# Reordering three places of a long mixer-and-feed-forward kernel: a causal attention's end, a linear attention's two rounds, and the last feed-forward phase

## The chip, the cores and the metric

The kernel runs on one core of one Trainium2 chip. A core has TensorE (PE in the profile; PEld is its weight load), VectorE (DVE), ScalarE (ACT), GpSimd (POOL) and SyncE (SP), which here issues almost all transfers. Each engine runs its own list of instructions in order; they meet only at semaphores (counters that one engine raises and another waits for). The metric is the device time of one execution in microseconds, the median of several runs.

## The reference

Two transformer blocks work on 512 tokens of width 1024, all in f32. The change lies in the second block:

```python
n = rms_norm_2(h, norm1_g);  proj = n @ w_in          # split into mq, mk, mv, gq, gk, gv, g_low, g_out, two gates
y_moba = moba_attention(mq, mk, mv, t5_bias)            # 8 heads of 64, causal, softmax with a T5 bias
log_a  = log_sigmoid(g_low @ gate_up + gate_bias) / 16
y_gla  = gla_attention(gq, gk, gv, log_a)               # 4 heads, keys 128, values 256, chunks of 64
y_gla  = rms_norm_2(y_gla, out_norm_g) * silu(g_out)
mixed  = sigmoid(gate_moba) * (y_moba @ w_branch_moba) + sigmoid(gate_gla) * (y_gla @ w_branch_gla)
h = h + mixed @ w_out
h = h + square(relu(rms_norm_2(h, norm2_g) @ w_up)) @ w_down       # 4096 hidden columns
```

With 512 tokens and blocks of 256, the selective attention comes to plain causal attention.

## The kernel before, in words

**Products.** Every f32 operand of a large product is kept as two parts: a high part rounded to fp32r (ACT copies it) and the rest, the low part (DVE or POOL subtracts). One product is then three matmuls into one PSUM bank, high by high, high by low, low by high: the helper `three` (lines 2328 to 2330). Activations lie transposed, 128 features by 512 tokens, so that a weight tile of 1024x128 is a product of 8 k-steps, 24 matmuls. A weight tile is loaded by SP into one of two slots of `w_raw` (`load_tile`, line 586), ACT makes `w_hi` (line 877), POOL makes `w_lo` (line 769), into one of four slots. `lo_done` counts finished low parts, `tile_done` finished products. No planner orders the work: the order of each engine is the order in which the code writes it out.

**Causal attention** (`scores`, `turn`, `output`, `gate`, `branch` on PE). For each head m and each query block q of 128: `scores` (two matmuls, lines 2789 and 2792, banks 4 and 5), DVE scales, adds the bias and takes the maximum (lines 1988, 1990), ACT exponentiates (1279), DVE divides (1995, 1996), `turn` transposes the probabilities on PE (2804, banks 6 and 7), ACT and DVE copy them out as high and low parts (1284, 2001). When all four blocks are turned, `output(m)` multiplies by the values (2814, 2815, bank m % 2); ACT and DVE take the result out as `y_hi`, `y_lo` (1290, 2008, 2009), counted by `o_lo`. Products that depend on none of this, the tiles of `gate_moba` (`gate(c, k0, k1)`, banks 2 and 3), are cut into k-steps and laid between the steps of the heads to keep PE busy. After head 7 come the four `branch` products (y_moba by w_branch_moba: two banks, 4*o + j, 4 k-steps each, so 24 matmuls; k-step k reads heads 2k and 2k+1), with the 16 matmuls of `g_low` (2866, 2867) between the second and third. These need `low_hi_and_lo`, which ACT and DVE make after ACT has copied the last gate tile, split a weight tile and applied eight sigmoids (lines 1258, 877, 1317, 1320, 2041).

**Linear attention.** A hardware loop of two rounds, two heads in each, `with pe.Fori(0, 2) as i`; ACT and DVE have loops of their own over the same rounds. A round computes four tiles of gq and gk (banks 4, 5, 0, 1), the values, the attention, and four tiles of g_out (`out_gate(j)`, banks 6, 7, 4, 5; ACT drains each by a SiLU and raises `y_s`), then transposes the output rows (`turn_rows`, 2931) and waits for the round's last `y_s` (4 and 8) as its last step. Behind the loop comes a loop of two rounds for the eight tiles of gate_gla (banks 4 to 7).

**Feed-forward.** Eight phases of 512 hidden columns. A phase has four `up` tiles (24 matmuls each; ACT applies relu and square) and a 2x2 block product in seven multiplications, M1, M2, M6, M5, M7, M4, M3 in PE's order (`down(n, x, p)`: two row blocks p, 6 matmuls each, bank `ff_bank(x, p)`: M1, M6, M7 share banks 0 and 1, M5 and M3 share 2 and 3). Operands of M5, M6, M7 and M3 are sums of blocks: M5 = a21 + a22, M6 = M5 - a11, M7 = a11 - a21, M3 = a12 - M6 (DVE's `hidden_sum`, counted by `f_sum`). ACT makes each high part (`hidden_hi`), DVE each low part (`hidden_lo`), in place of the sum where there was one. DVE adds each finished bank to the output rows (`add`, line 2273), each waiting for the one before (`f_add`), and M6, M7 and M3 on PE wait for the adds that free their banks: M6 for M1's, M7 for M6's, M3 for M5's. In the last phase M2 and M4 have banks and adds of their own, and SP stores finished rows (line 750). DVE does all four sums first, then all low parts, then the adds.

Of the kernel before, what the change touches and what calls it, by code (L numbers as in the profile page):

```python
# [20 lines left out]
P = 128  # L21
# [4 lines left out]
KC = D // P  # L26
# [5 lines left out]
HEADS = 8  # L32
# [10 lines left out]
MH = 8  # L43
# [92 lines left out]
def build(nc, d):  # L136
# [6 lines left out]
    with ctx:  # L143
# [14 lines left out]
        WH = at("w_hi", 56, [P, 4, KC * P], f32r)  # L158
# [140 lines left out]
        def bank(b, n=T, o=0):  # L299
            return PB[:, b * T + o:b * T + o + n]  # L300
# [172 lines left out]
        def ff_bank(x, p):  # L473

            return {M2: 4, M4: 6, M5: 2, M3: 2}.get(x, 0) + p

        def added(n, x, p=1):

# [394 lines left out]
        def _(act):  # L873
# [605 lines left out]
            def hidden_hi(n, x):  # L1479

                act.wait_ge(f_sq, HID * n + (2 if x == M1 else 4))
                if x in (M6, M5, M7, M3):
                    act.wait_ge(f_sum, 4 * n + {M5: 1, M6: 2, M7: 3, M3: 4}[x])
                plain = {M1: HF[:, 0:2, HALVES[0]], M2: HF[:, 2:4, HALVES[0]], M4: HF[:, 2:4, HALVES[1]]}
                act.activation(HAH[:, x, :, :], plain[x] if x in plain else HS[:, x, :, :], ACT.Copy).then_inc(f_hi, 1)

# [32 lines left out]
        def _(v):  # L1519
# [718 lines left out]
            def hidden_sum(n, x):  # L2238

                v.wait_ge(f_sq, HID * n + 4)  # L2240
                if x == M6 or x == M3:
                    v.wait_ge(f_sum, 4 * n + {M6: 1, M3: 2}[x])
                slot = lambda y: HS[:, y, :, :]
                if x == M5:
                    ins = v.tensor_tensor(slot(M5), a21, a22, ALU.add)
                elif x == M6:
                    ins = v.tensor_tensor(slot(M6), slot(M5), a11, ALU.subtract)
                elif x == M7:
                    ins = v.tensor_tensor(slot(M7), a11, a21, ALU.subtract)
                else:  # L2250
                    ins = v.tensor_tensor(slot(M3), a12, slot(M6), ALU.subtract)
                ins.then_inc(f_sum, 1)

            def hidden_lo(n, x):

                v.wait_ge(f_hi, 7 * n + x + 1)
                if x in (M6, M5, M7, M3):
                    v.wait_ge(f_sum, 4 * n + 4)
                src = {M1: a11, M2: a12, M4: a22}[x] if x in (M1, M2, M4) else HS[:, x, :, :]
                v.tensor_tensor(HAL[:, x, :, :], src, f(HAH[:, x, :, :]), ALU.subtract).then_inc(f_lo2, 1)  # L2260

# [2 lines left out]
            def add(n, x, p, m, half):  # L2264

                v.wait_ge(f_mm, ff_no(n, x, p))
                if n == 0 and x == M1 and p == 0:
                    v.wait_ge(r_copied, COPIED0 + 2 * TT)
                    v.wait_ge(c_rstd, RSTD0 + 3)
                if counted[0]:  # L2270
                    v.wait_ge(f_add, ADDED0 + counted[0])
                cols = slice(half * T, (half + 1) * T)
                v.scalar_tensor_tensor(ROWS[:, m, cols], bank(ff_bank(x, p)), RSC[:, m:m + 1], ROWS[:, m, cols], ALU.mult, ALU.add)\  # L2273
                    .then_inc(f_add, 1)
                counted[0] += 1
# [13 lines left out]
            for n in range(PHASES):  # L2289
                nxt = n < PHASES - 1  # L2290
                hidden_lo(n, M1)
                for x in (M5, M6, M7, M3):
                    hidden_sum(n, x)
                for x in range(1, 7):
                    hidden_lo(n, x)
                for p in range(2):
                    add(n, M1, p, p, 0)
                if not nxt:
                    for p in range(2):
                        add(n, M2, p, p, 0)  # L2300
                for p in range(2):
                    add(n, M6, p, p, 1)
                for p in range(2):
                    add(n, M5, p, p + 2, 1)
                if nxt:
                    down_sum(n + 1, M5)
                    down_sum(n + 1, M6)
                for p in range(2):
                    add(n, M7, p, p + 2, 0)
                    add(n, M7, p, p + 2, 1)  # L2310
                if nxt:
                    down_sum(n + 1, M7)
                    down_sum(n + 1, M4)
                else:
                    for p in range(2):
                        add(n, M4, p, p + 2, 0)
                for p in range(2):
                    add(n, M3, p, p, 1)
                if nxt:
                    for x in VECTOR_LO:  # L2320
                        low(n + 1, x)
# [3 lines left out]
        def _(pe):  # L2325
# [503 lines left out]
            for m in range(MH):  # L2829
                scores(m, 2, 4)  # L2830
                if m:
                    held = 4 if m < MH - 1 else 2
                    gate(m, held - 1, held)
                    output(m - 1)
                turn(m, 0)
                turn(m, 1)
                if m < MH - 1:
                    scores(m + 1, 0, 1)
                if m < MH - 1:
                    gate(m, 4, KC)  # L2840
                else:
                    gate(m, 2, 5)
                turn(m, 2)
                if m < MH - 1:
                    scores(m + 1, 1, 2)
                if m < MH - 1:
                    gate(m + 1, 0, 3 if m < MH - 2 else 1)
                turn(m, 3)
            gate(MH - 1, 5, 7)
            output(MH - 1)  # L2850
            gate(MH - 1, 7, KC)

            def branch(j):
                pe.wait_ge(lo_done, BM + j + 1)
                for o in range(2):
                    for k in range(4):
                        s = slice(2 * P * k + P * o, 2 * P * k + P * (o + 1))
                        mm = three(bank(4 * o + j), WH[:, j, s], WL[:, j, s], YH[:, k, :], YL[:, k, :], k == 0, k == 3)
                mm.then_inc(tile_done, 1)

            pe.wait_ge(o_lo, HEADS + MH)
            branch(0)
            branch(1)
            pe.wait_ge(l_lo, 1)
            for k in range(KC):
                pe.matmul(bank(7), LWS[:, k, :], UH[:, k, :], start=k == 0, stop=False)
# [9 lines left out]
                pe.wait_ge(bm_e, 2 * h + 1)  # L2876
                pe.matmul(bank(h), GUS[:, h * DK:(h + 1) * DK], GLS[:], start=True, stop=True).then_inc(l_up, 1)

            with pe.Fori(0, 2) as i:
                def attention(hh):  # L2880

                    n = 2 * i + hh
# [59 lines left out]
                        mm.then_inc(tile_done, 1)  # L2942

                for j in range(4):
                    if j == 2:
                        pe.wait_ge(l_abs, GH)
                        pe.wait_ge(on_done, 4 * i + 1)
                    product(tile_no(GK, i, j, 12), j, UH, UL, out=qk_bank(j))
# [28 lines left out]
                out_gate(3)  # L2977
                turn_rows(0)
                turn_rows(1)
                pe.wait_ge(y_s, 4 * i + 4)  # L2980

            with pe.Fori(0, 2) as i:
                for j in range(4):
                    if j == 2:
                        pe.wait_ge(go_rt, GH)
                    product(tile_no(GG, i, j), j, UH, UL, out=4 + j)
# [107 lines left out]
```

## Time and profile before

| | us |
|---|---|
| median of 3 runs | 1302.81 (1301.05 to 1306.74) |
| the profiled execution | 1301.05 |
| its span, first to last instruction | 1299.2 |
| PE busy in it | 1279.2 (98%) |
| DVE, ACT, POOL busy | 813.6, 657.0, 443.9 |
| DMA | 135.37 MB, mean 104 GB/s |

Busy times are of one execution; 1.85 us of its time lie outside the span. The stages that the change touches: causal attention from about 545 to 650 us of the span, the linear attention's rounds from 666 to 831 us, the last feed-forward phase's seven multiplications from 1273 us to the end. Matmul rows of PE overlap: a 128x512 matmul has a modelled duration of 0.39 us, while the next one starts about 0.23 us after it.

### The profile page before, as it was taken

To read this page: it belongs to the slowest core of one execution; us is meant where nothing else is said; L and a number is where in the kernel's file an instruction comes from. 1 tells how busy PE (TensorE), PEld (TensorE's weight loads), DVE (VectorE), ACT (ScalarE), POOL (GpSimd) and SP (SyncE) were. 2 spreads that over 40 slices of the span, in tenths; PEclk is the share of its full clock that TensorE was granted. 3 is DMA by queue.
4 is the path that set the end of the run, shared out by engine and by line. 5 is a ranking of instruction groups with operands and counts; after the bars stand their busy time and mean duration, and the time that the engine had idled before them with its cause. 6 is when DMAs were issued, how large, how long until landed. Compare 5 with 4: busy or idle time off the path is not lost.

```text
span 1299.2 us, 17513 instructions
## 1 busy us (share of the span) xinstructions
PE 1279.2 (98%) x6553; PEld 1066.6 (82%) x6553; DVE 813.6 (63%) x1215; ACT 657.0 (51%) x1074; POOL 443.9 (34%) x203
## 2 busy tenths in 40 slices
PE   8999999999999999999999999999999999999998
PEld 4688788889988888877689889888888888888886
DVE  1795788764935448778647325405448768667685
ACT  5553777844533354666654534633355544445341
POOL 0233011137432494422234333344563322332300
PEclk9999999999999999999999999999999999999999
DMA  9972001076332152321223322233255243332301
GB/s 349 313 238 74 11 23 33 18 242 198 90 91 65 45 167 81 100 63 49 64 65 98 82 81 68 72 102 97 82 161 159 84 126 102 101 111 81 114 1 65
DMA packets 181397, 135.37 MB, mean 104 GB/s; under 512 B 10154, under 2 KB 154651, under 8 KB 181324
## 3 DMA queue, kind: packets, MB, share of 16 engines
q1 hardware_dynamic: 181122, 134.34, 34.1%
q8 instruction: 46, 0.75, 0.3%
q14 instruction: 27, 0.22, 0.1%
q10 hardware_dynamic: 202, 0.06, 0.0%
HBM read 129.66 MB, written 4.72 MB: 103 GB/s over the span
## 4 chain that ended last, share of the span: by engine, by line
PE 88%; DVE 4%; ACT 3%; issue 2%; DMA 2%; POOL 1%; SPq 0%; DVEq 0%; ACTq 0%; POOLq 0%
PE psum L2328 27%; PE psum L2330 26%; PE psum L2329 26%; PE psum L2540 2%; DMA ada_w<-in_w_ada 1%; PE psum L2386 1%; PE psum L2530 1%; PE psum L2531 1%; POOL w_lo L769 1%; PE psum L2804 1%; PE psum L2792 1%; PE psum L2479 1%; ACT w_hi L877 0%; DMA w_raw<-in_w_in 0%; PE psum L2815 0%
## 5 line engine op out<-in xcount | busy, mean ns | idle before, releaser
L769 POOL TENSOR_TENSOR w_lo<-w_raw,w_hi 128x1024 fp32r<-128x1024 f32 x148 | 382.4, 2589 | 662.8 <-ACT w_hi L877 621.0
L2328 PE MATMUL psum<-u_hi,w_hi 128*128 128x512 f32 (+1 forms) x704 | 267.0, 379 | 1.7 <-ACT gated L1399 1.5
L2330 PE MATMUL psum<-u_hi,w_lo 128*128 128x512 f32 (+1 forms) x704 | 260.8, 370 | 0.0
L2329 PE MATMUL psum<-u_lo,w_hi 128*128 128x512 f32 (+1 forms) x704 | 260.7, 370 | 0.0
L877 ACT ACTIVATE w_hi<-w_raw 128x1024 fp32r<-128x1024 f32 x148 | 155.6, 1056 | 80.4 <-PE psum L2330 37.1
L2328 PE MATMUL psum<-y_hi,w_hi 128*128 128x512 f32 x416 | 162.2, 390 | 1.4 <-DVE y_lo L2009 1.4
L2329 PE MATMUL psum<-y_lo,w_hi 128*128 128x512 f32 x416 | 161.9, 389 | 0.0
L2330 PE MATMUL psum<-y_hi,w_lo 128*128 128x512 f32 x416 | 161.9, 389 | 0.0
L2328 PEld LDWEIGHTS psum<-u_hi,w_hi 128*128 128x128 f32 x704 | 132.7, 188 | 28.1 <-issue 4.4
L2330 PEld LDWEIGHTS psum<-u_hi,w_lo 128*128 128x128 f32 x704 | 132.7, 188 | 23.2
L2329 PEld LDWEIGHTS psum<-u_lo,w_hi 128*128 128x128 f32 x704 | 132.8, 189 | 20.6 <-issue 0.2
L2273 DVE SCALAR_TENSOR_TENSOR out_rows<-psum,row_rstd,out_rows 128x512 f32<-128x512 f32 x100 | 75.0, 750 | 39.5 <-PE psum L2330 34.8
L2328 PEld LDWEIGHTS psum<-y_hi,w_hi 128*128 128x128 f32 x416 | 78.1, 188 | 17.9 <-DVE y_lo L2009 1.8
L2330 PEld LDWEIGHTS psum<-y_hi,w_lo 128*128 128x128 f32 x416 | 78.1, 188 | 16.1
L2329 PEld LDWEIGHTS psum<-y_lo,w_hi 128*128 128x128 f32 x416 | 78.1, 188 | 16.1
L2328 PE MATMUL psum<-down_hi,hidden_hi 128*128 128x512 f32 x224 | 87.3, 390 | 2.7 <-DVE hidden_lo L2260 2.1
L2330 PE MATMUL psum<-down_hi,hidden_lo 128*128 128x512 f32 x224 | 87.2, 389 | 0.0
L1468 ACT ACTIVATE stage<-psum 128x512 f32<-128x512 f32 x32 | 19.0, 593 | 66.7 <-PE psum L2330 66.7
L2328 PEld LDWEIGHTS psum<-down_hi,hidden_hi 128*128 128x128 f32 x224 | 42.0, 188 | 12.2 <-issue 3.5
L1495 ACT ACTIVATE down_hi<-down_sum 128x1024 fp32r<-128x1024 f32 x24 | 24.6, 1057 | 53.9 <-DVE down_sum L2222 53.3
L2329 PE MATMUL psum<-down_lo_set,hidden_hi 128*128 128x512 f32 x128 | 49.8, 389 | 0.0
L793 POOL TENSOR_TENSOR w_lo<-w_raw,w_hi 128x768 fp32r<-128x768 f32 x8 | 14.8, 1846 | 102.4 <-ACT w_hi L981 102.4
(498 smaller groups left out, 2583.3 us busy)
## 6 DMA issues: line engine op xcount, KB each, us to landing
w_raw<-in_w_in SPq DMA_DIRECT2D x52, 512.0 KB, 3.8
w_raw<-in_w_up SPq DMA_DIRECT2D x32, 512.0 KB, 4.1
down_set<-in_w_down SPq DMA_DIRECT2D x32, 512.0 KB, 4.8
ada_back<-in_w_ada SPq DMA_DIRECT2D x7, 2048.0 KB, 10.3
w_raw<-in_fno_w_in SPq DMA_DIRECT2D x16, 512.0 KB, 4.0
ada_w<-in_w_ada SPq DMA_DIRECT2D x3, 2048.0 KB, 15.3
w_raw<-in_mla_w_in SPq DMA_DIRECT2D x11, 512.0 KB, 5.2
w_raw<-in_mla_w_out SPq DMA_DIRECT2D x8, 512.0 KB, 4.3
```

The costliest lines, as they stand in the source:

```text
L769: pool.tensor_tensor(WL[:, j, :], RAW[:, j % 2, :], f(WH[:, j, :]), ALU.subtract).then_inc(lo_done, 1)
L793: pool.tensor_tensor(WL[:, h % 4, 0:768], RAW[:, h % 2, 0:768], f(WH[:, h % 4, 0:768]), ALU.subtract).then_inc(lo_done, 1)
L877: act.activation(WH[:, j, :], RAW[:, j % 2, :], ACT.Copy).then_inc(hi_done, 1)
L1468: act.activation(E[:, t % 2, :], bank(up_bank(n, j)), ACT.Relu).then_inc(f_r, 1)
L1495: act.activation(WDH[:, x, :, :], down_raw(n, x)[:], ACT.Copy).then_inc(d_hi2, 1)
L2273: v.scalar_tensor_tensor(ROWS[:, m, cols], bank(ff_bank(x, p)), RSC[:, m:m + 1], ROWS[:, m, cols], ALU.mult, ALU.add)\
L2328: pe.matmul(out, ah, bh, start=first, stop=False, skip_group_check=more)
L2329: pe.matmul(out, ah, bl, start=False, stop=False, skip_group_check=more)
L2330: return pe.matmul(out, al, bh, start=False, stop=last, skip_group_check=more)
L2386: mm = pe.matmul(ada_row_bank(q)[0:2, :], CACT[:, k, :], AQ[q][:, k, :], start=k == 0, stop=k == KC - 1)
L2479: mm = pe.matmul(bank(5, 2, 2 * (4 * r + b)), ada_sum(r)[:, b * P:(b + 1) * P], ONES[:, 0:2], start=True, stop=True)
L2540: mm = pe.transpose(bank(2, P, k * P), PA[:, q % 2, k * P:(k + 1) * P], IDENT[:])
```

## The change

Three places, all of them order or waits; every product, sum and copy is still there once.

- **Last feed-forward phase.** DVE's order in the last phase becomes: sum M5, low M2, sum M6, sum M3, low M6, the two adds of M1, sum M7, low M5, M7, M4, M3, and then the adds as before. The numbers that ACT and DVE wait for follow the new order (`summed`); the low part of M6, made in place, waits for sum M3, the others for all four sums. The phases before are unchanged.
- **Causal attention.** In head 0, two of the gate tile's k-steps move ahead of the next head's first score block. In head 7 the gate tile's last three k-steps run ahead of `turn(7, 3)`. Behind it come the k-steps of the branch product that read heads 0 to 5: nine matmuls (tile 0, bank 0), then `output(7)`, then nine each for bank 4 and bank 5, then the wait for head 7's low part and the 21 other matmuls of tiles 0 and 1.
- **Linear attention.** PE's loop is written out twice (`for i in range(2)`), so that its waits are on constants. The wait for the round's last two SiLUs moves from the round's end to the products that write the drained banks: `y_s` 3 and 4 ahead of the second round's first two tiles, 7 ahead of the gate loop, 8 ahead of its second tile.

```diff
+        def summed(n, x):
+            return 4 * n + ((M5, M6, M3, M7) if n == PHASES - 1 else (M5, M6, M7, M3)).index(x) + 1
...
 # ACT, hidden_hi
-                    act.wait_ge(f_sum, 4 * n + {M5: 1, M6: 2, M7: 3, M3: 4}[x])
+                    act.wait_ge(f_sum, summed(n, x))
 # DVE, hidden_sum and hidden_lo
-                    v.wait_ge(f_sum, 4 * n + {M6: 1, M3: 2}[x])
+                    v.wait_ge(f_sum, summed(n, M5 if x == M6 else M6))
-                    v.wait_ge(f_sum, 4 * n + 4)
+                    v.wait_ge(f_sum, summed(n, M3) if n == PHASES - 1 and x == M6 else 4 * n + 4)
 # DVE, in the loop over the phases
+                else:
+                    hidden_sum(n, M5)
+                    hidden_lo(n, M2)
+                    hidden_sum(n, M6)
+                    hidden_sum(n, M3)
+                    hidden_lo(n, M6)
+                    for p in range(2):
+                        add(n, M1, p, p, 0)
+                    hidden_sum(n, M7)
+                    for x in (M5, M7, M4, M3):
+                        hidden_lo(n, x)
...
 # PE, causal attention
                 turn(m, 0)
                 turn(m, 1)
+                if m == 0:
+                    gate(m, 4, 6)
                 if m < MH - 1:
                     scores(m + 1, 0, 1)
                 if m < MH - 1:
-                    gate(m, 4, KC)
+                    gate(m, 4 if m else 6, KC)
                 else:
                     gate(m, 2, 5)
                 turn(m, 2)
+                if m == MH - 1:
+                    gate(m, 5, KC)
...
                 turn(m, 3)
-            gate(MH - 1, 5, 7)
-            output(MH - 1)
-            gate(MH - 1, 7, KC)
+            def branch_half(j, o, k0, k1):
+                for k in range(k0, k1):
+                    s = slice(2 * P * k + P * o, 2 * P * k + P * (o + 1))
+                    mm = three(bank(4 * o + j), WH[:, j, s], WL[:, j, s], YH[:, k, :], YL[:, k, :], k == 0, k == 3)
+                return mm
...
+            pe.wait_ge(lo_done, BM + 1)
+            pe.wait_ge(o_lo, HEADS + MH - 1)
+            branch_half(0, 0, 0, 3)
+            output(MH - 1)
+            pe.wait_ge(s_max, M0 + 4 * MH)
+            branch_half(0, 1, 0, 3)
+            pe.wait_ge(lo_done, BM + 2)
+            branch_half(1, 1, 0, 3)
             pe.wait_ge(o_lo, HEADS + MH)
-            branch(0)
-            branch(1)
+            branch_half(0, 0, 3, 4)
+            branch_half(0, 1, 3, 4).then_inc(tile_done, 1)
+            branch_half(1, 0, 0, 4)
+            branch_half(1, 1, 3, 4).then_inc(tile_done, 1)
...
 # PE, linear attention
-            with pe.Fori(0, 2) as i:
+            for i in range(2):
...
                 for j in range(4):
+                    if i and j < 2:
+                        pe.wait_ge(y_s, 3 + j)
...
                 turn_rows(1)
-                pe.wait_ge(y_s, 4 * i + 4)
-
+            pe.wait_ge(y_s, 7)
             with pe.Fori(0, 2) as i:
                 for j in range(4):
+                    if j == 1:
+                        pe.wait_ge(y_s, 8)
```

## Rows read from the trace of the kernel before

**Rows 1.** Page, parts 1 and 2: busy time by engine; clock in 40 slices.
```profile
PE 1279.2 (98%) x6553; PEld 1066.6 (82%) x6553; DVE 813.6 (63%) x1215; ACT 657.0 (51%) x1074; POOL 443.9 (34%) x203
...
PEclk9999999999999999999999999999999999999999
```

**Rows 2.** Waits of PE: who was waited for; us in total, times, longest.
```profile
PE psum L2328 <- DVE hidden_lo L2260: 2.1, 1, 2.1
...
PE psum L2328 <- ACT gated L1399: 1.5, 2, 0.8
...
PE psum L2328 <- DVE gv_lo L2110: 0.8, 1, 0.8
```

**Rows 3.** Timeline, head 0: start, duration, engine, line, tiles [idle before <- releaser].
```profile
557.82 0.44 PE L2804 MATMUL psum<-ident,m_probs 128*128 128x128 f32 x2 [0.17 <-DVE m_probs L1996]
...
559.15 0.30 PE L2789 MATMUL psum<-mk_lo_over_hi,mq_twice 128*128 128x128 f32 x1 [0.89 <-DVE m_stats L1990]
...
560.69 0.42 DVE L1996 TENSOR_SCALAR m_probs<-m_probs,neg_max 128x384 f32<-128x384 f32 x1
...
562.49 0.49 PE L2804 MATMUL psum<-ident,m_probs 128*128 128x128 f32 x3
```

**Rows 4.** Timeline, PE from head 7's third block to the product of g_low.
```profile
631.95 0.49 PE L2804 MATMUL psum<-ident,m_probs 128*128 128x128 f32 x3
...
633.77 0.66 PE L2804 MATMUL psum<-ident,m_probs 128*128 128x128 f32 x4 [1.34 <-DVE m_probs L1996]
...
639.46 0.51 PE L2328 MATMUL psum<-y_hi,w_hi 128*128 128x512 f32 x1 [1.39 <-DVE y_lo L2009]
...
650.49 0.39 PE L2866 MATMUL psum<-u_hi,low_hi_and_lo 128*128 128x512 f32 x1
```

**Rows 5.** The same stretch, ACT and DVE.
```profile
637.37 0.59 ACT L1290 ACTIVATE y_hi<-psum 64x512 fp32r<-64x512 f32 x1 [2.31 <-PE psum L2815]
...
638.12 0.60 ACT L1258 ACTIVATE mixed<-psum 128x512 f32<-128x512 f32 x1
...
645.16 0.83 ACT L1320 ACTIVATE low_hi_and_lo<-low_raw 128x768 fp32r<-128x768 f32 x1
...
646.03 0.42 DVE L2041 TENSOR_TENSOR low_hi_and_lo<-low_raw,low_hi_and_lo 128x256 fp32r<-128x256 f32 x1 [6.62 <-ACT low_hi_and_lo L1320]
```

**Rows 6.** Chain that ended last, ahead of the linear attention: start, us, what.
```profile
665.19 1.07 ACT w_hi L877
```

**Rows 7.** Timeline, end of the linear attention's first round.
```profile
746.22 1.91 PE L2931 MATMUL psum<-ident,o_rows 128*128 128x128 f32 x16
...
747.78 0.60 ACT L1399 ACTIVATE gated<-psum 128x512 f32 x1
...
748.92 0.49 PE L2328 MATMUL psum<-u_hi,w_hi 128*128 128x512 f32 x1 [0.80 <-ACT gated L1399]
```

**Rows 8.** Timeline, the last phase's seven multiplications.
```profile
1274.97 0.69 DVE L2245 TENSOR_TENSOR hidden_sum<-relu_squared 128x512 f32<-128x512 f32 x1 [6.97 <-ACT relu_squared L1473]
1275.76 0.69 DVE L2247 TENSOR_TENSOR hidden_sum<-hidden_sum,relu_squared 128x512 f32<-128x512 f32 x1
...
1278.18 1.89 DVE L2260 TENSOR_TENSOR hidden_lo<-hidden_sum,hidden_hi 128x512 fp32r<-128x512 f32 x3
...
1281.19 5.02 DVE L2273 SCALAR_TENSOR_TENSOR out_rows<-psum,row_rstd,out_rows 128x512 f32<-128x512 f32 x6
...
1296.00 0.75 DVE L2273 SCALAR_TENSOR_TENSOR out_rows<-psum,row_rstd,out_rows 128x512 f32<-128x512 f32 x1 [0.61 <-PE psum L2330]
...
1276.55 1.67 ACT L1485 ACTIVATE hidden_hi<-hidden_sum 128x512 fp32r<-128x512 f32 x3 [0.94 <-DVE hidden_sum L2247]
...
1278.41 0.47 PE L2328 MATMUL psum<-down_hi,hidden_hi 128*128 128x512 f32 x1 [2.05 <-DVE hidden_lo L2260]
...
1282.08 0.47 PE L2328 MATMUL psum<-down_hi,hidden_hi 128*128 128x512 f32 x1 [0.67 <-DVE out_rows L2273]
```

**Rows 9.** Page, part 6: transfers by line, count, KB each, us to landing.
```profile
w_raw<-in_w_in SPq DMA_DIRECT2D x52, 512.0 KB, 3.8
```

More of the change, by code:

```diff
@@ L2291, in _ @@
                 hidden_lo(n, M1)
[L2292 to L2297, printed above, removed]
+                if nxt:
+                    for x in (M5, M6, M7, M3):
+                        hidden_sum(n, x)
+                    for x in range(1, 7):
+                        hidden_lo(n, x)
[7 more added lines that the diff above has]
+                    hidden_lo(n, M6)
+                    for p in range(2):
+                        add(n, M1, p, p, 0)
+                    hidden_sum(n, M7)
+                    for x in (M5, M7, M4, M3):
+                        hidden_lo(n, x)
                 if not nxt:
@@ L2848, in _ @@
                 turn(m, 3)
-            gate(MH - 1, 5, 7)
-            output(MH - 1)
-            gate(MH - 1, 7, KC)
+            def branch_half(j, o, k0, k1):
[3 more added lines that the diff above has]
+                return mm
             def branch(j):
                 pe.wait_ge(lo_done, BM + j + 1)
[L2855 to L2859, printed above, removed]
+                branch_half(j, 0, 0, 4)
+                branch_half(j, 1, 0, 4).then_inc(tile_done, 1)
+            pe.wait_ge(lo_done, BM + 1)
[6 more added lines that the diff above has]
+            branch_half(1, 1, 0, 3)
             pe.wait_ge(o_lo, HEADS + MH)
-            branch(0)
-            branch(1)
+            branch_half(0, 0, 3, 4)
+            branch_half(0, 1, 3, 4).then_inc(tile_done, 1)
+            branch_half(1, 0, 0, 4)
+            branch_half(1, 1, 3, 4).then_inc(tile_done, 1)
             pe.wait_ge(l_lo, 1)
```

## The prediction

> **What bounds the kernel now.** I read the busy times first: PE is busy for 98% of the span and its clock stands at the higher of its two levels, 2.4 GHz, in all 40 slices [rows 1]. So no work of another engine is worth anything by itself; only PE's idle time is, some 20 us of 1299. Then the waits of PE, which say where it is lost: 2.1 us before one low part of the last phase, 1.5 us in two waits for a SiLU, 0.8 us for a low part of the values [rows 2]. Then the timeline around the three places, for what PE would do instead. Head 0 leaves 0.89 us idle [rows 3], the end of head 7 1.34 and 1.39 us [rows 4], the rounds' ends 0.80 and (1.5 less that) 0.7 us [rows 2, 7], the last phase 2.05 and 0.67 us [rows 8]: 7.8 us, the most that the change can aim at, give or take the slow first step behind each stop. The chain of waits is needed for one thing, whether time won before 665 us is kept.
>
> **The change part by part.** A scale first. From 639.46 to 650.49 us PE does 48 matmuls of 512 columns [rows 4], 0.23 us each. 16 transposes take 1.91 us with the last one's tail, 0.11 each [rows 7]. PE starts 0.14 us after the DVE add that it waits for has ended (1281.94 to 1282.08) [rows 8].
>
> *Head 0.* PE has done its two transposes at 558.06 and waits for the block maximum until 559.15 [rows 3]. Six gate matmuls in there (1.4, and 0.1 for the first) end at 559.55; the score block and the other six (0.5 and 1.5) end at 561.5, where the next transpose stood at 562.49. Its probabilities are ready at 560.69 + 0.42 = 561.11, in time. The first score block of head 1 comes 0.4 us later; DVE has until then the second block of head 0 to scale, so nothing waits for it. Gain 1.0; if head 1 is short of DVE, 0.5.
>
> *End of the causal attention.* The stretch from 631.95 to 650.49 is 18.54 us [rows 4]. In the new order PE does: 3 transposes 0.3, 9 gate matmuls 2.15, which carry it to 634.4, past the 633.77 at which the fourth block is there; 4 transposes 0.4; 9 branch matmuls 2.15; the output of head 7, 1.3 by its 2560 columns; 18 branch matmuls 4.15; 21 more 4.8. The sum is 15.25, so PE would be at the product of g_low at 647.2. Checks on the way: head 7's y_lo came 2.1 us behind ACT's start at 637.37, after one step of ACT and two of DVE [rows 4, 5]; ACT starts at 638.4 now, so it comes at 640.5, and PE asks at 642.4. Its turned low parts need one step of each, some 1.4 us behind the transposes' end at 635.0, so they come at 636.4, and PE asks at 636.9. The nine matmuls on either bank are thus cover enough.
> But another wait is now late. ACT's list is head 7's y_hi, the gate copy, a weight tile, eight sigmoids, `low_hi_and_lo`. y_hi starts 1.06 us later than at 637.37; the copy, which waited for PE until 638.12, follows at once, 0.55 behind, so the list is 0.85 later: `low_hi_and_lo` at 646.0 instead of 645.16, DVE's rest at 646.9 instead of 646.03, done at 647.3, and PE starts at 647.4 [rows 5]. So 0.2 us are given back, and the place gains 3.05. The transfers behind it (the small weights of g_low) are issued by SP after the same y_lo and so come 1.06 later; they landed before 645.16 by a margin that I leave open. Were there none, PE would start at 647.65. Bounds of the place: 2.8 to 3.3, and 1.3 if the second stop comes back in full.
> The weight tiles of the linear attention are split by ACT and POOL behind DVE's products with the branch results, 0.85 later as well; PE wants the first of them after 66 more matmuls, more than 14 us on, so they cost nothing. Is the time kept? The chain runs from PE's last branch product into ACT at 665.19 [rows 6], then through ACT, DVE and POOL to the wait of 0.8 us for the low part of the values [rows 2]. All of it is released by that branch product, so it moves along, and the wait keeps its size.
>
> *Linear attention.* The 16 transposes from 746.22 are done at 748.05; PE goes on at 748.92 [rows 7]. SiLU 2 of the round was long over, and SiLU 3 (747.78 + 0.60) is wanted only by the second tile, 5.4 us on. So 0.87 go, and by the second round's wait, 0.1 shorter [rows 2], 0.8: 1.65. The last SiLU ends 0.54 us before PE moves, not 0.14, so 0.40 in each gap is no semaphore; it is the loop's end, registers and branch. If it were a cost of the sequencer that stays, the gain would be 0.85; if it also falls away between tiles inside the rounds, 2.2. I take 1.65, since in the first round the branch itself is gone, and in the second PE has transposes queued meanwhile.
> The rule that bears on this is in the Trainium skill, "Runtime: NRT & Kernel Launch", section "Instruction fetch mechanics": a taken branch to a target outside the current window of instructions waits for a transfer of the target page, while straight code is fetched ahead. By it the 0.40 of the first round is a fetch that vanishes (sum as taken); without it 0.40 may stay and the sum is 0.4 less. No row here shows the fetch itself.
>
> *Last phase.* DVE steps: 0.60 for a sum or low part (three in 1.89 us, of 0.69 each), 0.79 where it reads its predecessor (1274.97 to 1275.76), adds 0.85 (six in 5.02); ACT starts 0.10 after the sum, steps 0.5 [rows 8]. New schedule: sum M5 1274.97; low M2 1275.65, as soon as ACT has its high part, done 1276.34; PE starts M2 at 1276.48 instead of 1278.41. Sum M6 1276.25, sum M3 1277.05, low M6 1277.83, first add of M1 1278.43, done 1279.18, so PE's M6 goes at 1279.32, just when M2's twelve matmuls (2.84) end: the stop at 1282.08 is gone, and PE is 2.75 ahead. Second add 1279.29; sum M7 1279.96; low M5 1280.75; then M7, M4 and M3 at 1281.4, 1282.0, 1282.6. PE's M6 and M5 run to 1284.85 without a stop. Only now, at 1283.2, come the adds of M2, and behind them those of M6 at 1284.9 and 1285.8, each 0.75. M7 on PE waits for the first: 1285.8. That is a new stop of 1.0 us, the price of the low parts between sums and adds. M7, M4 and M3 (36 matmuls, 8.2) then end at 1294.2, and DVE, with fourteen adds back to back from 1283.2, reaches its last at 1294.3 instead of 1296.00. Gain 1.7. The last four stores now follow each other by 0.85 us, and I charge 0.1 for that: 1.6. Bounds: 1.0 (each of seven DVE steps 0.1 slower) and 2.7 (no new stop).
>
> *Sum.* 1.0 + 3.05 + 1.65 + 1.6 = 7.3 us. The profiled execution took 1301.05, so 1293.8 of its kind; the median of the runs was 1.75 above it. I predict 1295.5.
>
> **The rivals.**
> *Half of it (4.5 us).* Stops come back where I count on margins of 0.1 to 0.5 us: in head 7 at y_lo or at `low_hi_and_lo` (3.05 becomes 1.8), at the loop (1.65 becomes 0.85), in the last phase (1.6 becomes 1.0), in head 0 (0.5) and 0.3 elsewhere. For it: the last phase is DVE-bound in my own schedule, with M6 at a margin of nothing. Against it: the stretches have no other late engine. 1298.3.
> *The edits of order do little (2 us).* PE's time is won but lost again at the 0.8 us wait for the values and behind it, if that chain hangs on a transfer and not on the branch product. Then 4.05 of the causal attention shrink to nothing, and 3.25 remain at most, 2 if the last phase gives 0.4. Against it: the chain's row at 665.19. 1300.8.
> *Slower: instruction fetch.* The second round on PE is new code: two rounds of some 517 matmuls and as many weight loads. If PE has to stop for the next piece of it, a stop is priced by the nearest transfer, 3.8 us to landing [rows 9], since none of an instruction page is shown; three of them are 11.4, with 7.3 won 4.1 more than before: 1306.9. It decides from two such stops on. Against it: the last phases are written out throughout, and none of PE's longer waits lies there but the two of this change.
>
> **How the numbers follow.** Forecast 0.58 (own range 1293.5 to 1297), half 0.27, little 0.08, slower 0.07. I call 0.5% (6.5 us, so below 1296.3 and above 1309.3) what a measurement can tell from no change. The forecast lies only 0.8 us beyond it. Faster gets the forecast's 0.58, though a tenth of it may end short of the bound and as much of the half case beyond; slower 0.04, since the fetch rival's 1306.9 counts as within until a fourth stop; within the other 0.38. The range, 1292.0 to 1301.5, takes in the upper bounds counted from the profiled execution (1301.05 - 9.2 = 1291.9), the half case and the little one, and leaves out the fetch.
>
> **What would show it.** In the profile after: no idle PE at the maximum of head 0; none before the branch products, about 0.2 us before line 2866 from DVE 2041; PE from transposes straight to the next tile at both rounds' ends; in the last phase one stop of about 1 us before M7, released by an add (2273), and less than 0.4 us before M2. Wrong would be: PE idle at those places, a longer wait for the values, or idle time inside the second round without a releaser (fetch).

## The result: 8 to 9 us less, and a little more than forecast

| | before | after |
|---|---|---|
| median of the first comparison | 1302.30 (1300.25 to 1306.74, 6 runs) | 1293.93 (1292.66 to 1296.07, 6 runs) |
| the profiled execution, its span | 1301.05, 1299.2 | 1294.15, 1292.4 |
| PE busy | 1279.2 (98%) | 1279.1 (99%) |
| second comparison, another five rounds | 1302.53 (1299.93 to 1304.73, 11 runs) | 1293.24 (1292.48 to 1295.01, 6 runs) |

The ratio is 0.9935, 95% interval 0.9922 to 0.9948, and in the second comparison 0.9931 (0.9919 to 0.9943): faster by 0.65 to 0.7%, a little more than the 0.5% that I had called measurable. Busy times hardly move (PE's by 0.1 us, DVE's from 813.6 to 816.0); what went is PE's idle time. The page of the changed kernel, which answers to [rows 1] and [rows 9]:

```profile
PE 1279.1 (99%) x6553; PEld 1067.3 (83%) x6553; DVE 816.0 (63%) x1215; ACT 656.4 (51%) x1074; POOL 443.2 (34%) x203
...
PEclk9999999999999999999999999999999999999999
...
w_raw<-in_w_in SPq DMA_DIRECT2D x52, 512.0 KB, 3.8
```

PE's waits after (who was waited for; us in total, times, longest), for [rows 2]:

```profile
PE psum L2344 <- DVE out_rows L2277: 0.8, 1, 0.8
PE psum L2344 <- DVE gv_lo L2114: 0.7, 1, 0.7
...
PE psum L2344 <- POOL w_lo L773: 0.5, 1, 0.5
PE psum L2820 <- DVE m_probs L2000: 0.4, 2, 0.2
```

The waits for the low part of M2, for the add before M6, for the two SiLUs, for head 7's fourth block and its `y_lo` and for head 0's maximum are gone. The wait for the values keeps its size, and a new one, 0.8 us for an add, stands before M7. The 0.5 us for a `w_lo` is at 303.76, in a stage that the change doesn't touch; 4 of the 14 profiled executions have it (0.2 to 0.5 us), and a second one of this kernel doesn't.

Head 0, PE, for [rows 3]: the gate products now stand where PE waited.

```profile
558.83 0.44 PE L2820 MATMUL psum<-ident,m_probs 128*128 128x128 f32 x2 [0.16 <-DVE m_probs L2000]
559.02 0.48 PE L2344 MATMUL psum<-u_hi,w_hi 128*128 128x512 f32 x1
...
560.50 0.22 PE L2805 MATMUL psum<-mk_lo_over_hi,mq_twice 128*128 128x128 f32 x1
...
562.40 0.49 PE L2820 MATMUL psum<-ident,m_probs 128*128 128x128 f32 x3
```

From head 7's third block to the product of g_low, PE, ACT and DVE, for [rows 4, 5]:

```profile
631.86 0.49 PE L2820 MATMUL psum<-ident,m_probs 128*128 128x128 f32 x3
...
634.26 0.60 PE L2820 MATMUL psum<-ident,m_probs 128*128 128x128 f32 x4
634.62 0.48 PE L2344 MATMUL psum<-y_hi,w_hi 128*128 128x512 f32 x1
...
638.20 0.60 ACT L1294 ACTIVATE y_hi<-psum 64x512 fp32r<-64x512 f32 x1 [2.70 <-PE psum L2831]
...
639.55 0.68 DVE L2013 TENSOR_TENSOR y_lo<-m_out_rest,psum 64x512 fp32r<-64x512 f32 x1
...
645.86 0.83 ACT L1324 ACTIVATE low_hi_and_lo<-low_raw 128x768 fp32r<-128x768 f32 x1
...
646.73 0.43 DVE L2045 TENSOR_TENSOR low_hi_and_lo<-low_raw,low_hi_and_lo 128x256 fp32r<-128x256 f32 x1 [6.49 <-ACT low_hi_and_lo L1324]
...
647.21 0.50 PE L2897 MATMUL psum<-u_hi,low_hi_and_lo 128*128 128x512 f32 x1
```

No releaser in brackets on PE's rows means no stop (of more than 0.15 us). `y_lo` is there at 640.23, and PE needs it only behind 27 branch matmuls; `low_hi_and_lo` ends at 647.16 and PE starts 0.05 later. So the last link is ACT's list, as forecast.

End of the linear attention's first round, for [rows 7]: the next tile starts before the third SiLU has ended (744.58 + 0.60 = 745.18).

```profile
743.01 1.91 PE L2962 MATMUL psum<-ident,o_rows 128*128 128x128 f32 x16
744.58 0.60 ACT L1403 ACTIVATE gated<-psum 128x512 f32 x1
...
744.68 0.48 PE L2344 MATMUL psum<-u_hi,w_hi 128*128 128x512 f32 x1
```

The last phase's DVE, for [rows 8]:

```profile
1269.78 0.69 DVE L2249 TENSOR_TENSOR hidden_sum<-relu_squared 128x512 f32<-128x512 f32 x1 [6.97 <-ACT relu_squared L1477]
1270.44 0.69 DVE L2264 TENSOR_TENSOR hidden_lo<-relu_squared,hidden_hi 128x512 fp32r<-128x512 f32 x1
...
1273.25 1.60 DVE L2277 SCALAR_TENSOR_TENSOR out_rows<-psum,row_rstd,out_rows 128x512 f32<-128x512 f32 x2
...
1278.02 11.87 DVE L2277 SCALAR_TENSOR_TENSOR out_rows<-psum,row_rstd,out_rows 128x512 f32<-128x512 f32 x14
...
1285.71 4.17 DVE L2277 SCALAR_TENSOR_TENSOR out_rows<-psum,row_rstd,out_rows 128x512 f32<-128x512 f32 x5
```

From 1278.02 on there are fourteen adds without a gap between them. The last row is the last five of them, from a shorter stretch; the last of the five starts at 1285.71 + 4.17 - 0.75 = 1289.13.

Spans differ by a microsecond or two in stages that both kernels share: ahead of head 0 the profiled execution of after is 1.01 us later (558.83 against 557.82), so the two spans lie only 6.8 us apart. So I compare distances between landmarks. The first three lines below are starts on PE; "transposes" are the sixteen at a round's end.

| from, to | before | after | gain | forecast |
|---|---|---|---|---|
| head 0: 2nd block's second transposes, 3rd block's | 4.67 | 3.57 | 1.10 | 1.0 |
| head 7's 3rd block, product of g_low | 18.54 | 15.35 | 3.19 | 3.05 |
| transposes, next tile; rounds 1 and 2 | 2.70, 2.63 | 1.67, 1.67 | 1.99 | 1.65 |
| last phase: first sum, last add (DVE) | 21.03 | 19.35 | 1.68 | 1.7 |
| last add's end, end of the span | 2.46 | 2.48 | -0.02 | -0.1 |

The sum is 7.9 us, against 7.3.

### The profile page after: what moved, and what is told of

It reads as the page before. It is cut to its first block, busy times and chain, and to the rows that moved or that the text cites. A ratio compares the mean times of both kernels' runs of the same rounds, so it can differ in the third digit from the quotient of the medians.

```text
span 1292.4 us, 17472 instructions
## 1 busy us (share of the span) xinstructions
PE 1279.1 (99%) x6553; PEld 1067.3 (83%) x6553; DVE 816.0 (63%) x1215; ACT 656.4 (51%) x1074; POOL 443.2 (34%) x203
## 4 chain that ended last, share of the span: by engine, by line
PE 87%; DVE 4%; ACT 3%; DMA 2%; issue 2%; POOL 2%; SPq 0%; DVEq 0%; POOLq 0%; ACTq 0%
PE psum L2344 26%; PE psum L2346 26%; PE psum L2345 26%; PE psum L2556 2%; POOL w_lo L773 1%; DMA ada_w<-in_w_ada 1%; PE psum L2402 1%; PE psum L2546 1%; DVE out_rows L2277 1%; PE psum L2547 1%; PE psum L2820 1%; PE psum L2808 1%; ACT w_hi L881 1%; PE psum L2831 0%; DMA w_raw<-in_mla_w_out 0%
```

## The experiments

All but two start from the changed kernel. Times without a range are single executions; their landmarks say more.

**The last phase alone undone.**

```diff
-            return 4 * n + ((M5, M6, M3, M7) if n == PHASES - 1 else (M5, M6, M7, M3)).index(x) + 1
+            return 4 * n + (M5, M6, M7, M3).index(x) + 1
...
-                if nxt:      # DVE: four sums, then all low parts, then the adds
+                if True:
```

> The changed kernel, but DVE's order in the last feed-forward phase (and the counts that ACT and DVE wait for) as before. Theory (each part's gain stands alone and is PE's idle time, less what comes back): from the first sum of the last phase to the start of the last add 21.0 us, as in the kernel before (the changed one has 19.4), PE idle 2.05 us before M2 and 0.67 before M6, none before M7, and everything ahead of the phase as in the changed kernel; span about 1.7 us longer than the changed one's. Rival (the last phase is bound by transfers or the stores' tail): the tail behind the last add changes by more than 0.3 us, or the span by less than 1.

1295.88 us. From first sum to last add 21.67 us, 2.3 more than after and 0.64 more than before; the other places keep their gains (1.67 at both rounds' ends), and the end of the span comes 2.46 us behind the last add's end, so the stores are not what changed. The stop of 2.05 us is back, the one of 0.67 before M6, which was expected too, is not; the surplus of 0.64 is not DVE's. PE in that execution, and one window of it (us, length, then busy time and count of PE, PEld, DVE, ACT and POOL, granted clock, DMA's share, GB/s):

```profile
1272.58 0.47 PE L2344 MATMUL psum<-down_hi,hidden_hi 128*128 128x512 f32 x1 [2.05 <-DVE hidden_lo L2264]
...
1274.31 0.63 PE L2344 MATMUL psum<-down_hi,hidden_hi 128*128 128x512 f32 x1
1274.74 0.63 PE L2345 MATMUL psum<-down_lo_set,hidden_hi 128*128 128x512 f32 x1
```
```profile
1274.00:1275.00 1.00, 1.00 (x4) 0.80 (x3) 1.00 (x3) 0.00 (x0) 0.00 (x0) 0.50 0.00 0
```

The granted clock is 0.50 of full speed, the lower level of 1.2 GHz. The matmuls follow each other by 0.43 instead of 0.23 us, from 1 us behind the stop until 1276.9. The place of the gain is settled by this run, its size is not (2.3 us, of which 0.64 are the clock's); and it raises the question to which the last four runs go.

**The causal attention's end undone.**

```diff
-                if m == MH - 1:
-                    gate(m, 5, KC)
...
+            gate(MH - 1, 5, 7)
+            output(MH - 1)
+            gate(MH - 1, 7, KC)
...
-            branch_half(0, 0, 0, 3)
-            output(MH - 1)
...
+            branch(0)
+            branch(1)
```

> The changed kernel, but the gate tile's last three k-steps and the branch products stand where they stood before (5 and 6 behind turn(7, 3), 7 behind the output of head 7, branch products behind head 7's low part). Theory: from turn(7, 2) to the product of g_low 18.5 us instead of 15.35, with idle stops of 1.3 and 1.4 us; the linear attention behind it unchanged in length, so that all 3.2 us stand in the span and the time is about 1297 us. Rival (the stages behind absorb it: the wait for the low part of the values at 697 us hangs on a transfer): that wait shrinks from 0.70 us by as much as PE is late, and the time stays within 1 us of the changed kernel's 1294.

1296.78 us (1295.92 to 1297.62, 4 runs), 0.9956 of before (0.9939 to 0.9973). The stretch is 18.53 us, before's 18.54. PE comes 3.2 us later than in the changed kernel, and its wait for the values is still 0.67 us, against 0.67 and 0.71 in the two executions of the changed kernel and 0.62 to 0.78 in the three of the kernel before. So time won ahead of it is kept, and the rival of "little" is dead.

**Only the gate steps early, the branch products as before.**

```diff
                 turn(m, 2)
                 if m == MH - 1:
                     gate(m, 5, KC)          # kept
...
-            branch_half(0, 0, 0, 3)
             output(MH - 1)
-            pe.wait_ge(s_max, M0 + 4 * MH)
-            branch_half(0, 1, 0, 3)
...
+            branch(0)
+            branch(1)
```

> The changed kernel with one half of the causal end alone: the gate tile's last three k-steps run ahead of turn(7, 3), but all branch matmuls wait behind head 7's low part. Theory: the stop of 1.3 us before turn(7, 3) is gone, but with no matmul left to lie behind turn(7, 3) the output of head 7 waits for its turned low parts (about 1.2 us) and the branch products for y_lo (about 2.1 us): 18.3 to 18.8 us from turn(7, 2) to the product of g_low, nothing gained. Rival (the two stops are separate, each edit removes its own): 17.1 us.

1298.05 us, and 20.69 us for the stretch: both numbers missed, though the two stops of the theory are there (1.41 us for about 1.2, 2.13 for about 2.1). PE's stops, and the clock behind the second:

```profile
634.99 0.50 PE L2830 MATMUL psum<-m_turned_hi,mv_pairs 128*128 128x512 f32 x1 [1.41 <-DVE m_turned_lo L2005]
...
638.61 0.62 PE L2344 MATMUL psum<-y_hi,w_hi 128*128 128x512 f32 x1 [2.13 <-DVE y_lo L2013]
...
639.03 0.63 PE L2345 MATMUL psum<-y_lo,w_hi 128*128 128x512 f32 x1
```
```profile
639.00:640.00 1.00, 1.00 (x4) 0.78 (x3) 0.00 (x0) 0.99 (x2) 1.00 (x1) 0.50 0.22 65
```

The stops together are 3.54 us instead of 2.73, which makes 8.03 us from the third block to the first branch product instead of 7.51: the gate steps are good for one wait and are then missed at the two others. The remaining 48 matmuls take 12.66 instead of 11.03 us, because about nine of them run at 1.2 GHz. 0.52 + 1.63 = 2.15, the whole difference to before. So the half edit is no gain even at full clock (19.06 us by this account), and the gain needs the branch products as cover.

**Head 0 undone.**

```diff
-                if m == 0:
-                    gate(m, 4, 6)
...
-                    gate(m, 4 if m else 6, KC)
+                    gate(m, 4, KC)
```

> The changed kernel, but the gate tile's k-steps of head 0 all behind head 1's first score block, as before. Theory: 0.89 us idle before that score block, 4.67 us from the transposes of head 0's second block to those of the third instead of 3.57, and the same 69.46 us from there to turn(7, 2): 1.1 us lost and not made up. Rival (DVE and ACT pace the heads behind it, and the win is used up there): the 69.46 us become shorter by as much.

1295.29 us; 4.67 us between the transposes, before's number, and 69.42 us from there to head 7 against 69.46. The 1.1 us are kept through all heads, against the rival.

**Second round written out, but with the waits where they were.**

```diff
-                    if i and j < 2:
-                        pe.wait_ge(y_s, 3 + j)
...
                 turn_rows(1)
+                pe.wait_ge(y_s, 4 * i + 4)
```

> The changed kernel with PE's two rounds written out, but the wait for the last SiLU at each round's end, as in the loop. It separates the wait from the loop. Theory (0.40 of the 0.54 us between the SiLU's end and PE's next matmul are the loop's registers and branch): 0.14 to 0.2 us there in the first round, so 2.3 us from the transposes' start to the next tile (2.70 in the loop, 1.67 in the changed kernel); in the second round, where a loop still begins behind the wait, more, up to 2.6. Rival (the delay is that of a semaphore and of the first weight load, whoever waits): 0.5 us and 2.7 in both rounds, and the inside of the rounds unchanged.

1295.09 us; 2.22 and 2.40 us from the transposes to the next tile. Round 1: the third SiLU ends at 744.22 + 0.60 = 744.82, PE starts at 744.87.

```profile
744.22 0.60 ACT L1403 ACTIVATE gated<-psum 128x512 f32 x1
...
744.87 0.50 PE L2344 MATMUL psum<-u_hi,w_hi 128*128 128x512 f32 x1 [0.31 <-ACT gated L1403]
```

0.05 us instead of the 0.54 of [rows 7]: the loop's end did cost 0.49 where PE had nothing queued. (At its stops for DVE, PE starts either 0.05 or 0.15 us behind the instruction that it waits for; if that holds for ACT too, up to 0.1 of the 0.49 may be that.) In round 2 the gap behind the SiLU is 0.23 instead of 0.47. With the waits at the end, writing out is thus worth 0.48 and 0.23 (2.70 - 2.22, 2.63 - 2.40), and moving them then 0.55 and 0.73.

**The loop kept, only the waits late.**

```diff
-            for i in range(2):
+            with pe.Fori(0, 2) as i:
...
+                    if j == 1:
+                        pe.wait_ge(y_s, 4 * i + 1)      # y_s starts at 1
...
                 turn_rows(1)
-
-            pe.wait_ge(y_s, 7)
+                pe.wait_ge(y_s, 4 * i + 4)
```

> The changed kernel with PE's hardware loop kept and only the waits moved to the products that need them (y_s is raised by one more at the start, by PE, so that each such wait is on a positive value; PE also loses nothing by it). Theory (what the loop costs is issue time of PE's sequencer, which lies beside the 16 queued transposes once nothing waits behind them): 1.7 us from the transposes' start to the next tile in both rounds, as in the changed kernel, so writing out the loop brings nothing. Rival (a taken branch stops PE's instruction stream, the instruction fetch of the forecast): 2.0 to 2.2 us in the first round.

1293.83 us; 1.66 and 1.67 us. Round 1:

```profile
742.73 1.91 PE L2963 MATMUL psum<-ident,o_rows 128*128 128x128 f32 x16
...
744.39 0.48 PE L2344 MATMUL psum<-u_hi,w_hi 128*128 128x512 f32 x1
```

The branch is back and costs nothing; what differs from the 0.49 us is that PE has its sixteen transposes queued while the sequencer takes it. A wait still stands at the round's end in this version, for the last SiLU but one; it had been met before PE came to it. So the late waits alone give all 1.99 us, and once they are there the written-out rounds add nothing.

**The adds of M6 ahead of those of M2.**

```diff
+                for p in range(2):
+                    add(n, M6, p, p, 1)      # now ahead of M2's
```

> The changed kernel with DVE's adds of M6 ahead of those of M2 in the last phase. Theory (the last phase is DVE-bound now: its fourteen adds run back to back): the stop of 0.78 us before M7 is gone and PE's last matmul comes 0.9 us earlier relative to the phase's first sum, but the last add still starts 19.4 us behind that sum; nothing gained. Rival (PE's stop is what the phase costs): the last add 0.9 us earlier, 18.5.

1292.68 us. M7's stop is gone and PE's last matmul comes 17.86 us behind the first sum (1268.30) instead of 18.86, but DVE's fourteen adds take as long as before and the last one stays at 19.35:

```profile
1276.54 11.87 DVE L2277 SCALAR_TENSOR_TENSOR out_rows<-psum,row_rstd,out_rows 128x512 f32<-128x512 f32 x14
```

DVE bounds this phase, and PE's stop of 0.78 us costs nothing.

**The same, and two low parts on POOL.**

```diff
+            for x, src in ((M4, HF[:, 2:4, HALVES[1]]), (M3, HS[:, M3, :, :])):
+                pool.wait_ge(f_hi, 7 * n + x + 1)
+                pool.wait_ge(f_lo2, 7 * n + x)
+                pool.tensor_tensor(HAL[:, x, :, :], src, f(HAH[:, x, :, :]), ALU.subtract).then_inc(f_lo2, 1)
...
-                    for x in (M5, M7, M4, M3):
+                    for x in (M5, M7):
```

> As the kernel with M6's adds first, and the low parts of M4 and M3 of the last phase are made by POOL, which is idle there, instead of DVE. Theory (DVE-bound): two steps of 0.6 us leave DVE, so the last add starts 18.3 to 18.4 us behind the first sum, where PE's last matmul becomes the bound; 1.0 us better than the changed kernel, about 1293 us. POOL needs 1.2 to 1.4 us for each; M4's must be there 12 us behind the first sum and is at 9. Rival (PE's order is what counts, DVE has slack): 18.5 already by the adds' order alone, and nothing more from POOL; or POOL's steps slow DVE's beside them and the gain is under 0.3.

1291.52 us (1291.34 to 1294.39, 4 runs), 0.9910 of before (0.9893 to 0.9926). POOL and the last add:

```profile
1275.35 1.30 POOL L880 TENSOR_TENSOR hidden_lo<-relu_squared,hidden_hi 128x512 fp32r<-128x512 f32 x1 [39.51 <-DVE hidden_lo L2271]
1276.80 1.29 POOL L880 TENSOR_TENSOR hidden_lo<-hidden_sum,hidden_hi 128x512 fp32r<-128x512 f32 x1
```
```profile
1286.35 0.75 DVE L2284 SCALAR_TENSOR_TENSOR out_rows<-psum,row_rstd,out_rows 128x512 f32<-128x512 f32 x1 [0.23 <-PE psum L2353]
```

1286.35 - 1268.07 = 18.28, 1.07 less than after. The two steps taken from DVE are worth 1.2; 0.13 of it is lost because PE is now the later one (the 0.23 in brackets).

**Both versions and the kernel before again, for the clock.**

> The kernel before, unchanged, profiled a second time, to see where TensorE's granted clock falls in an execution whose mean clock is below 1 (14 of its later executions had means of 0.996 to 1.000 and 1300.6 to 1305.6 us). Theory: the clock falls to 1.2 GHz for some 3.5 us right behind PE's longest stops, as in two of the experiments (behind a stop of 2.05 us in the last phase, 0.79 in the slice of 5 us, and behind one of 2.13 us at head 7), and each fall costs 1.5 to 1.9 us; so a slower execution of this kernel has them behind the stops of 2.05 us (last phase), 1.34 and 1.39 us (head 7) or at the head of the program. Rival: the falls lie anywhere, also where PE never stops, and have nothing to do with what the change takes away.

The first of the two: 1302.67 us, mean clock 0.997. While PE works, its clock is at 0.50 in two places only, behind head 0's stop and behind the last phase's. The first matmuls behind the two stops, and windows of both places:

```profile
558.63 0.30 PE L2789 MATMUL psum<-mk_lo_over_hi,mq_twice 128*128 128x128 f32 x1 [0.89 <-DVE m_stats L1990]
...
1279.38 0.47 PE L2328 MATMUL psum<-down_hi,hidden_hi 128*128 128x512 f32 x1 [2.06 <-DVE hidden_lo L2260]
```
```profile
559.00:559.85 0.85, 0.85 (x4) 0.69 (x5) 0.82 (x3) 0.66 (x4) 0.00 (x0) 1.00 0.90 269
559.90:563.25 3.35, 3.35 (x9) 2.65 (x8) 2.08 (x8) 1.31 (x4) 0.00 (x0) 0.50 0.02 5
563.35:564.35 1.00, 1.00 (x7) 0.71 (x5) 0.00 (x0) 0.27 (x1) 0.00 (x0) 1.00 0.00 0
...
561.00:563.00 2.00, 2.00 (x6) 1.52 (x6) 1.02 (x4) 0.50 (x2) 0.00 (x0) 0.50 0.03 8
...
1281.00:1283.00 2.00, 2.00 (x6) 1.56 (x5) 1.91 (x4) 0.00 (x0) 0.00 (x0) 0.50 0.00 0
```

Head 0 takes 6.25 us there instead of 4.67, the last phase 21.68 instead of 21.03 (most of the slow stretch is taken out of the stop before M6, which is then missing). The second execution had this expectation:

> As the run ahead of it, a third execution of the kernel before with a profile: same theory and rival. If both show a mean clock of 1.000, the place of the falls stays open and only their number per execution is known.

It took 1302.76 us, mean clock 0.998. Here the fall is at 143 us, at a stop of 1.30 us that all kernels have, and the last phase takes 21.02. So the theory holds for the first execution and fails for the second: a fall comes with a stop, but not with each, and not only with those that the change removes. Of four profiled executions with the stop of 2.05 us two had a fall behind it, of four with head 0's stop of 0.89 us one, of four with the two of 1.34 and 1.39 us none. Of all fourteen, three had one at 142 to 143 us (this one, the one with head 0 undone and one of the best version), and the one with the causal end undone had one at 11 us, at a wait of 0.75 us for a transfer. Eight of the fourteen also show 0.50 behind PE's last matmul, where it costs nothing and still lowers the mean.

The two other kernels, five rounds each:

> The changed kernel, unchanged, against the kernel before in five rounds. Theory: its mean clock stays at 0.999 or above, the kernel before's lies at 0.996 to 1.000, and part of the gain that its landmarks don't show (8.4 us by the medians, 6.8 by the two profiled spans) comes with the falls of the clock that the removed stops no longer cause; ratio 0.992 to 0.994. Rival: both kernels' clocks are alike and the difference is only the start of the execution; then the medians of executions at 1.000 differ by the same 8.4.

> The version with the last two low parts on POOL and the adds of M6 ahead of those of M2, beside the changed kernel on the same chip. Theory: 1.1 us less than the changed kernel by the last add's place (18.28 against 19.35 us behind the first sum), so a median 0.9 to 1.3 below it. Rival: no difference that the medians show (under 0.4 us).

After: 1293.24 us, ratio given above. The mean clocks of its 12 executions in both comparisons are 1.000 (eight), 0.999 (three) and 0.998 (one). Those of the kernel before, 25 timed beside the experiments, run from 0.996 to 1.000, mean 0.9974, and the time goes with them: 1304.83 on average at 0.996 (six), 1303.38 at 0.997 (eleven), 1300.93 at 1.000 (three). A slow stretch is 3.4 us long (559.90 to 563.25 above), which at half clock takes 0.0013 off the mean of 1300 us; by that estimate 0.9974 is two falls per execution and 0.9996 a third of one. At 1.000 alone, before is 1300.96 (four executions, the profiled one with them, spread over 1.95 us) and after 1293.11 (eight): 7.9 us, which agrees with the sum of the landmarks. The medians lie 8.4 and 9.3 apart. The best version: 1292.43 us (1291.19 to 1292.92, 5 runs), 0.9921 of before (0.9908 to 0.9933). That is 0.8 below the changed kernel beside it, just short of the 0.9 expected, and the intervals overlap; the landmark (18.29 against 19.35, in these two profiles as well) is the evidence for 1.07, the medians alone are not.

## Why the prediction was right, and where it was off

*Head 0, 1.0, measured 1.10.* Right in place and nearly in size; undone alone it gives back exactly 1.10.

*Causal attention, 3.05, measured 3.19.* The order of events is the forecast's: turned low parts at 636.22 (forecast 636.4), `y_hi` at 638.20 (638.4), `y_lo` at 640.23 (640.5), `low_hi_and_lo` at 645.86 (646.0), g_low at 647.21 (647.4), each one to three tenths early. Against the forecast's 647.4, 0.09 is the start at 631.86 instead of 631.95, which is no gain; another 0.09 is the hand-over from DVE to PE, for which I had charged 0.14 from an add and which took 0.05 here. ACT's list is the late link as said, and its price is small: 0.12 us of PE idle, or 0.28 if counted from 646.93, where the next matmul was due (646.70 + 0.23). What the margin of the small transfers was stays unused: `gate_up` is there when DVE asks.

*Linear attention, 1.65, measured 1.99.* This is the mis-sized term. I took 0.11 per transpose and the tail of the last, so 1.83 us for the sixteen; the next tile starts 1.67 behind their start, since it does not wait for the modelled end of the last one. That is 0.16 in each round, 0.32 of the 0.34. The 0.40 that I had given to the loop is real; it is 0.49 in the first round and 0.24 in the second by the run with the waits at the end. What I had wrong is why it goes: not because the branch is gone in the first round, but because PE has work queued. By the Trainium skill, "Runtime: NRT & Kernel Launch", section "Instruction fetch mechanics", a taken branch to code outside the window held would wait for a transfer. The page of the profile counts the transfers of instructions, and this is the row of the changed kernel:

```profile
q8 instruction: 50, 0.82, 0.3%
```

It is 46 packets and 0.75 MB in the kernel before and in the one with the loop kept, and 50 in every kernel with the rounds written out. Four more, of 16.4 KB each (0.82 MB by 50), fit one more copy of the round's code; had the loop fetched its body again, the counts should be alike. So the rule's stall has no transfer to stand on here, which leaves the loop's own instructions for the 0.49 us; that is argued, and which of them takes how long was not separated.

*Last phase, 1.7 less 0.1 for the stores, measured 1.68 less 0.02.* Event by event: the stop before M7 is 0.78 us instead of 1.0, and DVE has fourteen adds back to back. That DVE and not this stop sets the end was argued then and is shown now, by the run that removes the stop and leaves the last add where it is.

*The step to the median, +1.75, measured -0.2 and +0.8.* The sum was 7.3 and the profiled execution of after was to be 1293.8; I then added what the median of before lay above its profiled run, as if it would stay. It did not: the medians of after lie 0.2 below its profiled execution (1293.93 against 1294.15) and 0.8 above (1293.24 against 1292.48). The profiled execution of before was one at full clock, and of its 25 later ones, whose clocks are on record, only three were. The change removes stops (of 0.89 and 2.05 us) behind which the clock fell three times, in two profiled executions. This step and the surplus of the landmarks are why both medians lie at the lower end of my own range of 1293.5 to 1297, the second just below it. How much of the change of the mean clock (0.9974 to 0.9996) is owed to the removed stops is not shown: falls at 143 us and behind the last matmul count in it too, and two further profiles are few. That they can fall there, and what one costs, is shown.

*The rivals.* Half: at the margins of 0.1 to 0.5 us no stop came back but those forecast. (Its pieces, all taken together, leave 3.85 us and not the 4.5 that I gave it.) Little: dead by the 0.67 us before the values that stay when PE comes there 3.2 us later. Slower by instruction fetch: the rounds' insides (from the values' product that waits to the transposes in the first, from the first tile in the second) are 45.72 and 79.01 us as before, four more instruction transfers are there, and PE waits for none of them.

## What to carry to other kernels

Move a wait from a loop's end to the instruction that needs it, so that queued work lies in between: the wait may go as late as the buffer allows, and here the loop's own cost then hid behind that work, so that nothing needed to be written out. Independent work moved into a wait is only worth what is not missed where it stood; count every wait that it covered. And before adding the distance between a profiled run and the median to a forecast, look whether the granted clocks of the runs explain it, since a change of the stops changes that too.

## What the runs showed of the hardware

- PE's granted clock fell to 1.2 GHz at stops of 0.75, 0.89, 1.30, 2.05 and 2.13 us in some executions, and not in others of the same kernel. The eight falls lie between 0.2 us before PE's restart (at 143 us) and 1.3 us behind it (head 0). Seven or eight matmuls of 512 columns then follow each other by 0.43 instead of 0.23 us. One fall costs 1.6 us on a path that PE bounds, and 0.65 where a later stop takes it up. The Trainium skill, "TensorE: Matmul & The Clock Gate", section "Wait — 56ns, not 53.3ns?", gives 426.7 ns for this step at the lower level, which agrees, and 215.7 ns at the higher, where the traces show 0.227 us; the traces decide.
- The way back in a hardware loop cost PE 0.49 us when it stood behind a wait (0.1 of it in doubt, see there), and nothing when sixteen transposes were queued; leaving it, 0.24.
- The subtraction of 128x512 takes POOL 1.30 us and DVE 0.69 (0.60 from start to start where they don't depend on each other).
- From the end of a DVE instruction to PE's start there were either 0.05 or 0.15 us at every stop of the three places and at the wait for the values. It is not a property of the semaphore: at the wait for the values it is 0.05 in the four executions with PE's hardware loop and 0.15 in the ten with the rounds written out. What decides it stays open.
